# A hybrid attention layer on one core: a new order in the first tile, and the product with the state from f16 pairs

## Chip, core, metric

The kernel runs on one core of one Trainium2 chip. The metric is the device time of one execution in microseconds, the median of several runs. TensorE (PE) multiplies, VectorE (DVE) and ScalarE (ACT) do elementwise work, GpSimd (POOL) does almost nothing here, and SyncE (SP) issues nearly all DMAs.

## What is computed

One layer of an encoder is applied to a prompt of 4096 tokens and to a sample of 64 tokens, in f32, width 1024:

```python
shift, scale, gate = split(silu(c) @ w_ada + b_ada, 3)
h    = rmsnorm(x, g_pre) * (1 + scale) + shift
proj = h @ w_in                 # 2832 columns: gq gk gv gg ga | sq sk sv sg
# GLA: 4 heads, dk 64, dv 128, a gate per token and channel
log_a = log_sigmoid(ga @ w_alpha + b_alpha) / 16
S_t  = diag(exp(log_a_t)) S_{t-1} + k_t^T v_t ;  o_t = q_t S_t
o_gla = rmsnorm(o) * silu(gg)
# SWA: 8 query heads, 2 key heads, window = own and previous chunk of 64, a sink per head
o_swa = softmax_with_sink(rope(sq) rope(sk)^T / 8) sv * silu(sg)
y    = x + gate * rmsnorm(concat(o_gla, o_swa) @ w_out, g_post)
```

Outputs are y for both, the GLA states behind both, and the key and value caches.

## The kernel before

**Tiles.** The prompt is cut into 32 tiles of 128 tokens. Tiles 0 and 1 are written out (`first` and `second` in the program; 0 to 3 on ScalarE), a loop runs two tiles at a time, tiles 30 and 31 are written out again; then come `sample()` and `after()`. Every engine has its own program, an instruction list in a fixed order with waits on named semaphores; nothing is planned by a scheduler.

**Pairs.** A matmul of f32 accuracy is made of f16 pairs: each operand is split into an upper half (`hi`, a copy to f16, mostly on ScalarE) and a lower one (`lo`, the difference, on VectorE), and the three products hi·hi, hi·lo, lo·hi are added in PSUM (`split_product`). The weights are split the same way while they arrive: `split_hi` on ScalarE counts the semaphore `w_half`, `split_lo` on VectorE counts `w_split`. One product was left in f32: q_int times the state S, in `gla_out`, two matmuls of 256 columns a tile; S holds two heads side by side with zeros in the other head's rows.

**A tile on PE**, in order: q and k of GLA (`qk_mm`, 96 matmuls of 128 columns); `gla_out` of the *previous* tile; the projections `W_KSG` (272 columns) and `W_SQ`; a transpose of the gate input; `values` (softmax weights times v) and `state_product` of the previous tile; `W_V`; z; `W_GG`; `W_SG`; the scores; the transposes of k_out and the products q·k of GLA (`a_mm`); the output projection of the previous tile (`out_mm`, 48 matmuls of 512 columns). In tile 0 `modulation(2)`, the gate's part of the adaLN, stands where there is no output projection.

**A tile on VectorE**: `make_h` (h of the next tile), scaling of y, the gates of the previous tile (waits for `o_rs` from ScalarE), the residual, `ga_lo` and `v_lo` (semaphore `vb_lo`, which PE awaits ahead of its transpose), `h_tok_lo`, rope, `mix_swa`, `s_update` (the state), `mix_lo`, `v_keys`, the lower q/k pairs (`pair_lo`), `v_ev`, the gate's running sum `scan`, exponents and factors (`bc_d`, `fac_d`), the scaled q and k (`qk_d`, then `k_off`, `q_int`, `k_out`: `gla_sc`), a copy of the keys (`k_ev`), the gate of gg (add one, reciprocal, multiply: `gg_x`), the maxima of the scores up to `m_neg`, the masking (`a_masked`), the gate of sg (reciprocal; in the middle of it `at_d`, the lower halves of A and k, semaphore that PE awaits ahead of the next tile), `p_lo`, denominators, `sg_g`. Both gates use the one buffer `etmp`.

**ScalarE** makes squares and roots, upper halves, exponentials; near a tile's end: the exponentials of gg and sg, the softmax (8 exponentials), `p_hi`, and then `at_hi`, the upper halves of A and k.

**SyncE** issues in the order of its list. In a tile: store of y, load of the residual, transposes of h (`turn_h`, by DMA), of q and k (`turn_heads`), the load of x for the tile after next, the transposes of the mix (`turn_mix`, which the output projection awaits), of the softmax weights (`turn_probs`). In tile 0 the loads of the last four adaLN units and of w_out stand among these.

Of the kernel before, what the change touches and what calls it, by code (L numbers as in the profile page):

```python
# [29 lines left out]
MID0, MID1 = 32, 96  # L30
P_SHIFT = 15.0 * math.log(2.0)
# [22 lines left out]
UNITS += [("ada", GATE_UNIT + i, slot) for i, slot in enumerate((4, 5, 6, 3))]  # L54
# [32 lines left out]
def hybrid_layer(nc, x_prompt, x_sample, c_prompt, c_sample, state_gla, cache_k, cache_v, w_ada, b_ada, g_pre,  # L87
# [3 lines left out]
    with ctx:  # L91
# [74 lines left out]
        q_int, k_out = lsp, la  # L166
# [6 lines left out]
        S = sb("S", [P, 2, 2, DV])  # L173
# [114 lines left out]
        def _(sp):  # L288
# [56 lines left out]
            def store_state(t, st):  # L345
                sp.wait_ge(sem["s_upd"], t)
                for q in range(2):
                    sp.dma_start(st[0, 0].rearrange("(b q) k v -> q k b v", q=2)[q],
                                 S[DK * q:DK * q + DK, :, q, :]).then_inc(sem["out_stored"], 16)

# [73 lines left out]
            def sample():  # L424
# [8 lines left out]
                for q in range(2):  # L433
                    sp.dma_start(S[DK * q:DK * q + DK, :, q, :],
                                 state_gla[0, 0].rearrange("(b q) k v -> q k b v", q=2)[q]).then_inc(sem["state_in"], 16)
# [46 lines left out]
        def _(pe):  # L482
            def split_product(out, a, b):

                for c in range(KC):
                    for n, (i, j) in enumerate(((0, 0), (0, 1), (1, 0))):
                        last = pe.matmul(out, a(c, i), b(c, j), start=(c == 0 and n == 0),  # L487
                                         stop=(c == KC - 1 and n == 2))
                return last
# [97 lines left out]
            def program(c):  # L587
# [5 lines left out]
                def project(bank, width, col, done):  # L593

                    if c.first:
                        pe.wait_ge(w_split, in_units_before[col])
                    split_product(bank[:, 0:width], h,
                                  lambda cc, i: (w_hi, w_lo)[i][:, cc, col:col + width]).then_inc(done, 1)
# [9 lines left out]
                for b in range(4):  # L608
                    if c.first and b % 2 == 0:
                        pe.wait_ge(w_split, b // 2 + 1)  # L610
                    last = split_product(qk_ch[:, b, :],
                                         lambda cc, i: (w_hi, w_lo)[i][:, cc, W_QK + b * P:W_QK + (b + 1) * P], h)
# [120 lines left out]
            def sample():  # L733
# [62 lines left out]
                pe.wait_ge(sem["state_in"], 16 * 2)  # L796
                for b in range(2):
                    pe.matmul(o_gla_s[:, 2 * b * DV:2 * (b + 1) * DV], q_int[:, b, 0:CHUNK], S[:, b, :, :],
                              start=True, stop=False)
# [70 lines left out]
        def _(act):  # L870
# [108 lines left out]

            def program(c):  # L980
# [38 lines left out]
                if c.first:  # L1019
                    split_hi([("in", 8), ("in", 9)])  # L1020
# [28 lines left out]
                if c.first:  # L1049
                    split_hi([("in", 10), ("in", 11)])  # L1050
# [38 lines left out]
                act.wait_ge(sem["a_masked"], t + 1)  # L1089
                act.activation(aT[0:64, 0, :, :, :], qk_d[0:64, :, :, :], ACT.Copy)  # L1090
                act.activation(aT[64:128, 0, :, :, 64:128], qk_d[64:128, :, :, 64:128], ACT.Copy)
                act.activation(k_tok[:, 0, :, :], kt_ps, ACT.Copy).then_inc(sem["at_hi"], 1)
# [100 lines left out]
        def _(dve):  # L1193
# [116 lines left out]
            def s_update(t):  # L1310
                dve.wait_ge(sem["u_mm"], t)
                for q in range(2):
                    r = slice(DK * q, DK * (q + 1))
                    for b in range(2):
                        last = dve.scalar_tensor_tensor(S[r, b, q, :], S[r, b, q, :], fac[r, b, 5:6],
                                                        u_ps[r, b, :], ALU.mult, ALU.add)
                last.then_inc(sem["s_upd"], 1)

# [26 lines left out]
            def y_scale(n, buf):  # L1345
                dve.wait_ge(sem["y_rs"], n)
                dve.scalar_tensor_tensor(y_buf[buf], pairP[:, :], y_r[:, :], gate_row, ALU.mult, ALU.mult)\
                   .then_inc(sem["y_mul"], 1)

            def program(c):  # L1350
# [39 lines left out]
                if c.prev:  # L1390
# [7 lines left out]
                                      mix_tok[:, :, 0, :], ALU.subtract).then_inc(sem["mix_lo"], 1)  # L1398
                if c.second:
# [8 lines left out]
                if c.first:  # L1408
                    make_h(c)
# [15 lines left out]
                dve.wait_ge(sem["scan"], t + 1)  # L1425
                refs = bsum[:, :, :].rearrange("p b (h k) -> p b h k", h=2)[:, :, :, MID0:MID0 + 1]
# [4 lines left out]
                dve.tensor_copy(fac_in[:, :, 0:2], ref2)  # L1431
# [15 lines left out]
                if c.last:  # L1447
# [4 lines left out]
                dve.tensor_tensor(halves(q_int), halves(q_d),  # L1452
                                  fac[:, :, 0:2].unsqueeze(3).to_broadcast([P, 2, 2, CHUNK]), ALU.mult)
# [12 lines left out]
                dve.wait_ge(sem["gg_e"], t + 1)  # L1466
                dve.tensor_scalar(etmp[:, :], etmp[:, :], 1.0, None, ALU.add).then_inc(sem["gg_1"], 1)
                dve.wait_ge(sem["gg_1"], t + 1)
                dve.reciprocal(etmp[:, :], etmp[:, :]).then_inc(sem["gg_r"], 1)  # L1469
                dve.wait_ge(sem["gg_r"], t + 1)  # L1470
                dve.scalar_tensor_tensor(gates[:, 0:512], bank6[:, :], DESCALE, etmp[:, :], ALU.mult, ALU.mult)\  # L1471
                   .then_inc(sem["gg_x"], 1)

# [28 lines left out]
                for q in range(2):  # L1502
# [5 lines left out]
                last.then_inc(sem["a_masked"], 1)  # L1508

# [4 lines left out]
                dve.wait_ge(sem["at_hi"], t + 1)  # L1514
                dve.tensor_tensor(aT[0:64, 1, :, :, :], qk_d[0:64, :, :, :], aT[0:64, 0, :, :, :], ALU.subtract)
                dve.tensor_tensor(aT[64:128, 1, :, :, 64:128], qk_d[64:128, :, :, 64:128],
                                  aT[64:128, 0, :, :, 64:128], ALU.subtract)
                dve.tensor_tensor(k_tok[:, 1, :, :], kt_ps, k_tok[:, 0, :, :], ALU.subtract).then_inc(sem["at_d"], 1)  # L1518
                dve.wait_ge(sem["sg_r"], t + 1)
                for ch in range(2):  # L1520
# [7 lines left out]
                dve.wait_ge(sem["p_hi"], t + 1)  # L1528
                dve.tensor_tensor(pair_tok[:, 1, :], late[:, 0:D], pair_tok[:, 0, :], ALU.subtract)\
                   .then_inc(sem["p_lo"], 1)  # L1530
# [10 lines left out]
            def sample():  # L1541
# [36 lines left out]
                dve.tensor_copy(fac_in[:, :, 0], bsum[:, :, MID0])  # L1578
# [13 lines left out]
                dve.tensor_tensor(q_int[:, :, c0], q_d[:, :, c0], fac[:, :, 0:1].to_broadcast([P, 2, CHUNK]), ALU.mult)  # L1592
# [11 lines left out]
                dve.tensor_copy(vA_s[c0, :, :], vB[c0, 0, :, :]).then_inc(sem["v_keys"], 1)  # L1604
                dve.wait_ge(sem["a_mm"], t + 1)
# [86 lines left out]
        def _(pool):  # L1692
# [15 lines left out]
            pool.memset(S[:, :, :, :], 0.0).then_inc(sem["scan_m"], 1)  # L1708
# [46 lines left out]
```

## Time and profile before

| | us |
|---|---|
| median of 3 runs | 1537.49 (1537.09 to 1538.28) |
| the profiled execution | 1537.71 |
| its span, first to last instruction | 1536.0 |
| PE busy | 1491.2 (97%) |
| DVE busy | 1151.2 (75%) |
| ACT busy | 634.5 (41%) |
| a tile of the loop | 44.7 |

All times in the views count from the start of the span. A matmul's end is modelled, since matmuls overlap; their starts tell the pace. In the chain of waits each piece is the work that the end waited for at that time.

### The profile page before, as it was taken

The page shows a single profiled execution, that of the slowest core. Times are in us where ns is not written, and L with a number is a line of the kernel's source. Part 1 is how long each engine was busy: PE and PEld are TensorE (multiplying, and loading weights), DVE is VectorE, ACT ScalarE, POOL GpSimd, SP SyncE. Part 2 cuts the span into 40 slices and gives each one's busy share as a digit, 9 for nine tenths or more (in the row PEclk, how much of TensorE's full clock was granted, in tenths as well). Part 3 has the DMA queues.
Part 4 walks back from the last instruction along what each step waited for, and adds up shares of the span by engine and source line. Part 5 has one row for each costly group of instructions (what it writes and reads, how often), then busy time and mean ns, then how long its engine had stood idle before and what let it go on. Part 6 is the DMA issues. An engine that isn't in the chain of part 4 may idle for free.

```text
span 1536.0 us, 31114 instructions
## 1 busy us (share of the span) xinstructions
PE 1491.2 (97%) x12204; PEld 872.2 (57%) x12204; DVE 1151.2 (75%) x2262; ACT 634.5 (41%) x1905; POOL 7.1 (0%) x17
## 2 busy tenths in 40 slices
PE   4789999999999999999999999999999999999997
PEld 3455556566555656655565665556566555656653
DVE  1889877777887777788777778877777887777775
ACT  2735443444444344344434434443443434344343
POOL 1000000000000000000000000000000000000000
PEclk9889999999999999999999999999999999999999
DMA  9982333323233332323333232333323243432334
GB/s 318 302 219 67 89 84 93 81 67 86 58 91 80 92 84 65 89 53 92 79 92 85 65 89 51 92 79 92 89 61 89 51 92 79 92 90 63 68 49 102
DMA packets 305388, 144.53 MB, mean 94 GB/s; under 512 B 266769, under 2 KB 291690, under 8 KB 305354
## 3 DMA queue, kind: packets, MB, share of 16 engines
q1 hardware_dynamic: 304768, 143.92, 38.8%
q8 instruction: 22, 0.36, 0.1%
q10 hardware_dynamic: 586, 0.15, 0.0%
q14 instruction: 12, 0.10, 0.0%
HBM read 63.08 MB, written 17.56 MB: 53 GB/s over the span
## 4 chain that ended last, share of the span: by engine, by line
PE 92%; DVE 4%; DMA 1%; ACT 1%; issue 1%; SPq 0%; ACTq 0%; DVEq 0%
PE bank L487 59%; PE pairP L487 20%; PE pairQ L549 2%; PE pairQ L674 2%; PE pairQ L566 2%; PE pairQ L554 1%; PE pairQ L576 1%; DMA w_hi<-in_w_ada 1%; PE bank L500 1%; PE bank L717 1%; PE bank L652 1%; PE bank L684 1%; DMA hT<-pair_tok 1%; PE bank L680 0%; DVE etmp L1469 0%
## 5 line engine op out<-in xcount | busy, mean ns | idle before, releaser
L487 PE MATMUL bank<-w_hi,hT 128*128 128x512 f16 (+1 forms) x2576 | 719.5, 360 | 7.8 <-DVE w_lo L1236 7.8
L487 PE MATMUL bank<-w_lo,hT 128*128 128x512 f16 (+2 forms) x1288 | 462.9, 359 | 0.0
L487 PEld LDWEIGHTS bank<-w_hi,hT 128*128 128x128 f16 x2576 | 252.5, 98 | 255.3 <-issue 10.1
L487 PE MATMUL pairP<-wo,late 128*128 128x512 f16 x1488 | 326.6, 379 | 0.0
L487 PEld LDWEIGHTS pairP<-wo,late 128*128 128x128 f16 x1488 | 143.0, 98 | 170.4
L487 PE MATMUL bank<-hT,w_hi 128*128 128x128 f16 (+1 forms) x2112 | 182.0, 221 | 10.3 <-DVE k_tok L1518 5.8
L487 PEld LDWEIGHTS bank<-w_lo,hT 128*128 128x128 f16 (+1 forms) x1288 | 126.3, 98 | 114.6 <-issue 0.8
L487 PE MATMUL bank<-hT,w_lo 128*128 128x128 f16 (+1 forms) x1056 | 179.9, 221 | 0.0
L487 PEld LDWEIGHTS bank<-hT,w_hi 128*128 128x128 f16 x2112 | 164.3, 99 | 18.7 <-issue 6.7
L1361 DVE SCALAR_TENSOR_TENSOR gates<-pairQ,o_r,gates 128x128 f32<-128x128 f32 x124 | 34.9, 345 | 109.0 <-ACT o_r L900 109.0
L1079 ACT ACTIVATE late<-pairQ,m_neg 128x128 f32<-128x128 f32 (+1 forms) x256 | 89.6, 376 | 58.9 <-DVE m_neg L1495 58.9
L1469 DVE RECIPROCAL etmp<-etmp 128x512 f32<-128x512 f32 x32 | 107.3, 3353 | 1.1
L1513 DVE RECIPROCAL etmp<-etmp 128x512 f32<-128x512 f32 x32 | 107.3, 3353 | 1.1
L487 PEld LDWEIGHTS bank<-hT,w_lo 128*128 128x128 f16 x1056 | 104.4, 99 | 0.0
L991 ACT ACTIVATE junk<-pairQ 128x128 f16<-128x128 f32 x124 | 32.5, 277 | 165.3 <-PE pairQ L554 165.3
L1069 ACT ACTIVATE etmp<-bank 128x512 f32<-128x512 f32 x32 | 19.1, 597 | 156.3 <-DVE gates L1471 146.3
L1327 DVE TENSOR_TENSOR etmp<-qk_tok,trig_in 128x80 f32<-128x80 f32 (+1 forms) x33 | 8.0, 242 | 93.3 <-ACT qk_tok L1014 93.0
L1014 ACT ACTIVATE qk_tok<-bank 128x512 f32<-128x512 f32 x32 | 19.1, 597 | 112.2 <-PE bank L487 112.2
L975 ACT ACTIVATE stage<-pairP 128x1024 f32<-128x1024 f32 x32 | 32.8, 1024 | 76.6 <-PE pairP L487 75.5
L1025 ACT ACTIVATE pair_tok<-gates 128x1024 f16<-128x1024 f32 x31 | 32.8, 1057 | 66.0 <-DMA hT<-pair_tok 64.3
L1079 ACT ACTIVATION_READ_ACCUMULATOR late<-pairQ,m_neg 128x1 f32 x256 | 55.4, 217 | 0.0
L1525 DVE SCALAR_TENSOR_TENSOR gates<-bank,etmp 64x256 f32<-64x256 f32 x128 | 53.6, 419 | 1.3
(300 smaller groups left out, 1939.4 us busy)
## 6 DMA issues: line engine op xcount, KB each, us to landing
x_in<-in_x_prompt SPq DMA_DIRECT2D x32, 512.0 KB, 3.5
x_res<-in_x_prompt SPq DMA_DIRECT2D x32, 512.0 KB, 4.2
out<-stage SPq DMA_DIRECT2D x32, 512.0 KB, 3.1
wo<-in_w_in SPq DMA_DIRECT2D x8, 1024.0 KB, 11.4
w_hi<-in_w_ada SPq DMA_DIRECT2D x4, 1024.0 KB, 9.1
w_lo<-in_w_ada SPq DMA_DIRECT2D x4, 1024.0 KB, 12.6
wo<-in_w_ada SPq DMA_DIRECT2D x4, 1024.0 KB, 7.3
late<-pair_tok SPq DMA_TRANSPOSE x160, 3.2
```

Source lines behind the costliest of these rows:

```text
L487: last = pe.matmul(out, a(c, i), b(c, j), start=(c == 0 and n == 0), stop=(c == KC - 1 and n == 2))
L549: pe.matmul(o_ps[:, 2 * b * DV:2 * (b + 1) * DV], q_int[:, b, :], S[:, b, :, :], start=True, stop=False)
L566: last = pe.matmul(pv_ps[:, k * HD:(k + 1) * HD], pair_ch[:, i, k, :], v[:, j, HD * g:HD * (g + 1)], start=(n == 0), stop=(n == 2))
L674: last = pe.matmul(scores[:, 4 * g + 2 * ch + pp, :], qT[:, ch, head:head + 2, :], kk[:, g, part, :], start=(part == 0), stop=(part == 1))
L975: act.activation(y_buf[buf], pairP[:, :], ACT.Square, accum_out=y_ss[:, :]).then_inc(sem["y_sq"], 1)
L991: last = act.activation(junk[:, hd * DV:(hd + 1) * DV], o_ps[:, hd * DV:(hd + 1) * DV], ACT.Square, accum_out=o_ss[:, hd:hd + 1])
L1025: act.activation(mix_tok[:, :, 0, :], gates[:, :].rearrange("p (f k) -> p f k", f=2), ACT.Copy)\
L1079: act.activation(probs[:, g, 0:w], scores[:, g, 0:w], ACT.Exp, bias=m_neg[:, g:g + 1], scale=HD ** -0.5, accum_out=row_sum[:, g:g + 1])
L1361: last = dve.scalar_tensor_tensor(gates[:, o], o_ps[:, o], o_r[:, hd:hd + 1], gates[:, o], ALU.mult, ALU.mult)
L1469: dve.reciprocal(etmp[:, :], etmp[:, :]).then_inc(sem["gg_r"], 1)
L1513: dve.reciprocal(etmp[:, :], etmp[:, :]).then_inc(sem["sg_r"], 1)
L1525: last = dve.scalar_tensor_tensor(gates_swa[CHUNK * e:CHUNK * (e + 1), :, ch, :, :], heads[0], DESCALE, heads[1], ALU.mult, ALU.mult)
```

## The change

Two things are changed together.

*State product.* S is kept once, without the zeros (`[P, 2, 128]`), and a pair of f16 halves of S/8 in the layout with zeros (`S_pair`) beside it. `s_hi` and `s_lo` make the halves each tile, `s_hi` behind `mix_lo`, `s_lo` behind the scan. q_int becomes a pair too (upper half, an f32 copy `q_tmp` in the place of bsum, lower half as the difference); the factor 8 is put into its exponent. `gla_out` multiplies three f16 pairs of 256 columns in place of one f32 pair.

*Order.* In tile 0 PE adds all products with the weights' upper halves first and waits for the lower halves (`w_split`) only then. ScalarE splits unit 10 earlier. VectorE's `make_h` goes behind the splits of units 10 and 11; the gate of gg goes behind `p_lo`, ahead of the gate of sg, whose exponential moves behind `p_hi`. In tiles 0 and 1 `at_hi` stands ahead of the softmax and `at_lo` ahead of the gate of sg. The last adaLN unit is loaded into slot 1, not 3.

```diff
+S_SCALE = 8.0
-UNITS += [("ada", GATE_UNIT + i, slot) for i, slot in enumerate((4, 5, 6, 3))]
+UNITS += [("ada", GATE_UNIT + i, slot) for i, slot in enumerate((4, 5, 6, 1))]
...
-        q_int, k_out = lsp, la
+        q_int = lsp[:, :, :].bitcast(F16).rearrange("p b (s k) -> p b s k", s=2)
+        q_tmp, k_out = bsum, la
-        S = sb("S", [P, 2, 2, DV])
+        S = sb("S", [P, 2, DV])
+        S_pair = sb("S_pair", [P, 2, 2, 2, DV], F16)
...
+            def upper_first(out, operands, units):
+                pe.wait_ge(w_half, units)
+                for c in range(KC):
+                    for i in range(2):
+                        pe.matmul(out, *operands(c, i, 0), start=(c == 0 and i == 0), stop=False)
+                pe.wait_ge(w_split, units)
+                for c in range(KC):
+                    last = pe.matmul(out, *operands(c, 0, 1), start=False, stop=(c == KC - 1))
+                return last
...
             def gla_out():
                 for b in range(2):
-                    pe.matmul(o_ps[:, 2 * b * DV:2 * (b + 1) * DV], q_int[:, b, :], S[:, b, :, :],
-                              start=True, stop=False)
+                    for n, (i, j) in enumerate(((0, 0), (0, 1), (1, 0))):
+                        pe.matmul(o_ps[:, 2 * b * DV:2 * (b + 1) * DV], q_int[:, b, i, :], S_pair[:, j, b, :, :],
+                                  start=(n == 0), stop=False)
```

ScalarE:

```diff
                 if c.first:
-                    split_hi([("in", 8), ("in", 9)])
+                    split_hi([("in", 8), ("in", 9), ("in", 10)])
...
                 if c.first:
-                    split_hi([("in", 10), ("in", 11)])
+                    split_hi([("in", 11)])
...
-                act.wait_ge(sem["sg_mm"], t + 1)
-                act.wait_ge(sem["gg_x"], t + 1)
-                act.activation(etmp[:, :], bank7[:, :], ACT.Exp, scale=-DESCALE).then_inc(sem["sg_e"], 1)
+                if not c.first:
+                    sg_exp(t)
+                if c.first or c.second:
+                    at_hi(t)
                 act.wait_ge(sem["m_neg"], t + 1)
...
                 act.activation(pair_tok[:, 0, :], late[:, 0:D], ACT.Copy).then_inc(sem["p_hi"], 1)
...
+                if c.first:
+                    sg_exp(t)
+                if not (c.first or c.second):
+                    at_hi(t)
```

VectorE (`gg_gate`, `at_lo`, `p_lo` hold the lines that stood in the program, unchanged):

```diff
+            def s_hi():
+                for q in range(2):
+                    r = slice(DK * q, DK * (q + 1))
+                    last = dve.tensor_scalar(S_pair[r, 0, :, q, :], S[r, :, :], 1.0 / S_SCALE, None, ALU.mult)
+                return last
+
+            def s_lo():
+                for q in range(2):
+                    r = slice(DK * q, DK * (q + 1))
+                    last = dve.scalar_tensor_tensor(S_pair[r, 1, :, q, :], S[r, :, :], 1.0 / S_SCALE,
+                                                    S_pair[r, 0, :, q, :], ALU.mult, ALU.subtract)
+                return last
...
                     dve.tensor_tensor(mix_tok[:, :, 1, :], gates[:, :].rearrange("p (f k) -> p f k", f=2),
                                       mix_tok[:, :, 0, :], ALU.subtract).then_inc(sem["mix_lo"], 1)
+                    dve.wait_ge(sem["s_upd"], t)
+                    s_hi()
...
                    .then_inc(sem["pair_lo"], 1)
-                if c.first:
-                    make_h(c)
...
                 dve.wait_ge(sem["scan"], t + 1)
+                if c.prev:
+                    s_lo()
...
-                dve.tensor_copy(fac_in[:, :, 0:2], ref2)
+                dve.tensor_scalar(fac_in[:, :, 0:2], ref2, TAU * math.log(S_SCALE), None, ALU.add)
...
                 if c.first:
                     split_lo([("in", 10), ("in", 11)])
+                    make_h(c)
...
-                dve.tensor_tensor(halves(q_int), halves(q_d),
-                                  fac[:, :, 0:2].unsqueeze(3).to_broadcast([P, 2, 2, CHUNK]), ALU.mult)
+                by_half = fac[:, :, 0:2].unsqueeze(3).to_broadcast([P, 2, 2, CHUNK])
+                dve.tensor_tensor(q_int[:, :, 0, :].rearrange("p b (h k) -> p b h k", h=2), halves(q_d), by_half,
+                                  ALU.mult)
+                dve.tensor_tensor(halves(q_tmp), halves(q_d), by_half, ALU.mult)
...
                 dve.tensor_copy(kA[:, :, :, 0:CHUNK], kB[:, :, :, 0:CHUNK]).then_inc(sem["k_ev"], 1)
+                dve.wait_ge(sem["gla_sc"], t + 1)
+                dve.tensor_tensor(q_int[:, :, 1, :], q_tmp[:, :, :], q_int[:, :, 0, :], ALU.subtract)
                 if c.first:
                     h_tok_lo(c)
...
+                if not c.first:
+                    gg_gate(t)
...
                 last.then_inc(sem["a_masked"], 1)
+                if c.first or c.second:
+                    at_lo(t)
+                if c.first:
+                    p_lo(t)
+                    gg_gate(t)
```

The sample on VectorE, behind `a_masked` and behind the reciprocal, and POOL:

```diff
+                dve.wait_ge(sem["state_in"], 16 * 2)
+                s_hi().then_inc(sem["state_in"], 1)
...
+                dve.wait_ge(sem["state_in"], 16 * 2 + 1)
+                s_lo().then_inc(sem["state_in"], 1)
                 dve.wait_ge(sem["sc_mm"], t + 1)
...
+            pool.memset(S_pair[:, :, :, :, :], 0.0)
+            pool.memset(S[:, :, :], 0.0).then_inc(sem["scan_m"], 1)
```

In the sample the state is loaded by a DMA into S (`state_in`), PE's product there uses the pairs as in `gla_out`, and q_int is made as in a tile.

## Rows read from the trace of the kernel before

**Rows 1.** The page: busy time of the engines, and the chain that ended last.

```profile
PE 1491.2 (97%) x12204; PEld 872.2 (57%) x12204; DVE 1151.2 (75%) x2262; ACT 634.5 (41%) x1905; POOL 7.1 (0%) x17
...
PE 92%; DVE 4%; DMA 1%; ACT 1%; issue 1%; SPq 0%; ACTq 0%; DVEq 0%
```

**Rows 2.** Stretches: length, busy PE, PEld, DVE, ACT, POOL (x), PEclk, DMA share, GB/s.

```profile
95.00:100.00 5.00, 5.00 (x64) 5.00 (x62) 4.78 (x8) 0.00 (x0) 0.00 (x0) 0.66 0.96 355
233.50:278.20 44.70, 44.70 (x367) 26.07 (x365) 33.92 (x68) 18.28 (x57) 0.00 (x0) 1.00 0.34 79
847.00:848.00 1.00, 1.00 (x18) 0.88 (x17) 0.40 (x1) 0.51 (x1) 0.00 (x0) 1.00 0.00 0
1505.00:1506.00 1.00, 1.00 (x12) 0.41 (x8) 0.03 (x1) 0.00 (x0) 0.00 (x0) 1.00 0.00 0
```

**Rows 3.** Who waited for whom: us in total, times, longest.

```profile
PE bank L487 <- DVE w_lo L1236: 7.8, 3, 5.3
PE bank L487 <- DVE k_tok L1518: 5.8, 2, 4.6
```

**Rows 4.** The chain of waits in order of time: start, us, what.

```profile
94.38 7.15 PE bank L487 x96
...
103.17 2.79 PE bank L487 x24
...
143.92 5.52 PE bank L487 x96
...
194.16 0.49 PE pairQ L549 x2
194.64 0.33 PE pairQ L554 x6
...
849.08 10.47 PE pairP L487 x48
...
1506.97 0.48 DVE qk_d L1608 x2
```

**Rows 5.** Timeline of VectorE in tiles 0 and 1: start, us, operation, [idle before].

```profile
67.44 1.28 DVE L1264 SCALAR_TENSOR_TENSOR late<-x_in,x_r,xs 128x1024 f32<-128x1024 f32 x1
...
76.71 0.42 DVE L1440 SCALAR_TENSOR_TENSOR qk_d<-bank,qk_d 128x256 f32<-128x256 f32 x1
...
79.79 0.42 DVE L1467 TENSOR_SCALAR etmp<-etmp 128x512 f32<-128x512 f32 x1
80.24 3.35 DVE L1469 RECIPROCAL etmp<-etmp 128x512 f32<-128x512 f32 x1
...
85.42 0.17 DVE L1478 MEMSET late<- 128x128 f32 x1 [1.10 <-PE pairQ L674]
...
98.15 1.28 DVE L1264 SCALAR_TENSOR_TENSOR late<-x_in,x_r,xs 128x1024 f32<-128x1024 f32 x1
...
104.95 1.13 DVE L1361 SCALAR_TENSOR_TENSOR gates<-pairQ,o_r,gates 128x128 f32<-128x128 f32 x4 [4.26 <-ACT o_r L900]
```

**Rows 6.** Timeline of ScalarE in tile 0: softmax, p_hi, at_hi.

```profile
87.44 0.32 ACT L1079 ACTIVATE late<-pairQ,m_neg 128x64 f32<-128x64 f32 x1 [2.37 <-DVE m_neg L1495]
...
90.25 1.06 ACT L1088 ACTIVATE pair_tok<-late 128x1024 f16<-128x1024 f32 x1
91.22 0.61 ACT L1090 ACTIVATE aT<-qk_d 64x512 f16<-64x512 f32 x1
```

**Rows 7.** Timeline of VectorE in a tile of the loop.

```profile
832.16 1.23 DVE L1315 SCALAR_TENSOR_TENSOR S<-S,fac,pairQ 64x128 f32<-64x128 f32 x4
...
837.17 0.69 DVE L1414 SCALAR_TENSOR_TENSOR v_raw<-bank,v_raw 128x512 f16<-128x512 f32 x1 [0.46 <-ACT v_raw L1037]
...
842.02 0.42 DVE L1452 TENSOR_TENSOR lsp<-qk_d,fac 128x256 f32<-128x256 f32 x1
...
848.23 0.69 DVE L1484 TENSOR_REDUCE smax<-pairQ 128x4 f32<-128x512 f32 x1 [0.83 <-PE pairQ L674]
...
856.55 0.42 DVE L1518 TENSOR_TENSOR k_tok<-bank,k_tok 128x256 f16<-128x256 f32 x1
```

More of the change, by code:

```diff
@@ L608, in program @@
                 for b in range(4):
[L609 to L612, printed above, removed]
+                    cols = slice(W_QK + b * P, W_QK + (b + 1) * P)
+                    if c.first:
+                        last = upper_first(qk_ch[:, b, :], lambda cc, i, j: ((w_hi, w_lo)[j][:, cc, cols], h(cc, i)),
+                                           b // 2 + 1)
+                    else:
+                        last = split_product(qk_ch[:, b, :], lambda cc, i: (w_hi, w_lo)[i][:, cc, cols], h)
                 last.then_inc(sem["qk_mm"], 1)
@@ L795, in sample @@
                 pe.wait_ge(sem["p_exp"], t + 1)
-                pe.wait_ge(sem["state_in"], 16 * 2)
+                pe.wait_ge(sem["state_in"], 16 * 2 + 2)
                 for b in range(2):
-                    pe.matmul(o_gla_s[:, 2 * b * DV:2 * (b + 1) * DV], q_int[:, b, 0:CHUNK], S[:, b, :, :],
-                              start=True, stop=False)
+                    for n, (i, j) in enumerate(PRODUCTS):
+                        pe.matmul(o_gla_s[:, 2 * b * DV:2 * (b + 1) * DV], q_int[:, b, i, 0:CHUNK],
+                                  S_pair[:, j, b, :, :], start=(n == 0), stop=False)
                     for q in range(2):
@@ L1348, in y_scale, with p_lo, gg_gate, at_lo @@
                    .then_inc(sem["y_mul"], 1)
+            def p_lo(t):
+                dve.wait_ge(sem["p_hi"], t + 1)
+                dve.tensor_tensor(pair_tok[:, 1, :], late[:, 0:D], pair_tok[:, 0, :], ALU.subtract)\
+                   .then_inc(sem["p_lo"], 1)
+            def gg_gate(t):
+                dve.wait_ge(sem["gg_e"], t + 1)
+                dve.tensor_scalar(etmp[:, :], etmp[:, :], 1.0, None, ALU.add).then_inc(sem["gg_1"], 1)
+                dve.wait_ge(sem["gg_1"], t + 1)
+                dve.reciprocal(etmp[:, :], etmp[:, :]).then_inc(sem["gg_r"], 1)
+                dve.wait_ge(sem["gg_r"], t + 1)
+                dve.scalar_tensor_tensor(gates[:, 0:512], bank6[:, :], DESCALE, etmp[:, :], ALU.mult, ALU.mult)\
+                   .then_inc(sem["gg_x"], 1)
+            def at_lo(t):
+                dve.wait_ge(sem["at_hi"], t + 1)
+                dve.tensor_tensor(aT[0:64, 1, :, :, :], qk_d[0:64, :, :, :], aT[0:64, 0, :, :, :], ALU.subtract)
+                dve.tensor_tensor(aT[64:128, 1, :, :, 64:128], qk_d[64:128, :, :, 64:128],
+                                  aT[64:128, 0, :, :, 64:128], ALU.subtract)
+                dve.tensor_tensor(k_tok[:, 1, :, :], kt_ps, k_tok[:, 0, :, :], ALU.subtract).then_inc(sem["at_d"], 1)
             def program(c):
@@ L1508, in program @@
                 last.then_inc(sem["a_masked"], 1)
+                if c.first or c.second:
+                    at_lo(t)
+                if c.first:
+                    p_lo(t)
+                    gg_gate(t)
                 dve.wait_ge(sem["sg_e"], t + 1)
@@ L1513, in program @@
                 dve.reciprocal(etmp[:, :], etmp[:, :]).then_inc(sem["sg_r"], 1)
[L1514 to L1518, printed above, removed]
+                if not (c.first or c.second):
+                    at_lo(t)
                 dve.wait_ge(sem["sg_r"], t + 1)
@@ L1527, in program @@
                 last.then_inc(sem["sg_x"], 1)
-                dve.wait_ge(sem["p_hi"], t + 1)
-                dve.tensor_tensor(pair_tok[:, 1, :], late[:, 0:D], pair_tok[:, 0, :], ALU.subtract)\
-                   .then_inc(sem["p_lo"], 1)
+                if not c.first:
+                    p_lo(t)
                 dve.wait_ge(sem["p_exp"], t + 1)
@@ L1604, in sample @@
                 dve.tensor_copy(vA_s[c0, :, :], vB[c0, 0, :, :]).then_inc(sem["v_keys"], 1)
+                dve.wait_ge(sem["gla_sc"], t + 1)
+                dve.tensor_tensor(q_int[:, :, 1, c0], q_tmp[:, :, c0], q_int[:, :, 0, c0], ALU.subtract)
                 dve.wait_ge(sem["a_mm"], t + 1)
```

37 lines of the change are left out of this document (19 added, 18 removed).

## The prediction

> **What bounds the kernel now.** I read the shares of the chain that ended last first, then the busy time by stretch, then that chain in order of time, then who waited for whom, and last the VectorE and ScalarE timelines of the first two tiles and of one tile of the loop. TensorE (PE) carries 92% of the chain and is busy 97% of the span [rows 1]. In a tile of the loop it is busy for all 44.70 us of 44.70 while VectorE (DVE) works 33.92 [rows 2]: from about 144 us on, a microsecond saved on PE is a microsecond of the kernel, and work added to DVE is free as long as no PE wait comes to end late. Ahead of that it is otherwise: PE waits 7.8 us for the lower halves of the weights and 5.8 us for DVE's `k_tok` [rows 3], which is the end of the work that hands a tile over (semaphore `at_d`). After the second of these waits the clock falls: 0.66 of full speed between 95 and 100 us [rows 2], and the same 96 matmuls take 7.15 us where they take 5.52 at tile 2 [rows 4]. So there are three terms: the loop (PE), the first two tiles (DVE and ScalarE in turn with PE), and the end (the sample, where the chain runs through DVE).
>
> **The state product, in the loop.** One f32 matmul of 256 columns (two records) takes 0.49 us on the chain, and six f16 ones of 128 columns take 0.33, or 0.056 each [rows 4]. The change puts three f16 matmuls of 256 columns in place of each. No such row exists. Two of 128 columns would be 0.112; the 24 matmuls of 272 columns take 2.79 us, 0.116 each, which is an upper end, and scaled by 256/272 they give 0.109 [rows 4]. I take 0.110, so 0.33 in place of 0.49: 0.16 saved, with ends 0.14 and 0.163. There are two products a tile, and PE sets the time at 31 of the 32 places (tiles 2 to 31 and the sample; tile 1 belongs to the front). 62 x 0.16 = **9.9 us less** (8.7 to 10.1). Their weights are as wide as those of the other f16 matmuls, whose loads lie under matmuls half as long.
>
> The row is dearer than a count of passes makes it: four passes at 0.110 would be 0.44, and 62 x 0.11 only 6.8 us. That count is the Trainium skill's, "FP8 and Floating Point Precision", section "TensorE Precision Notes": a true FP32 product goes through the array four times. By that rule three passes in place of four save a quarter; the trace, with 0.49 us, says a third. The measurement decides, and the quarter is a rival below.
>
> **What DVE pays for it in the loop.** New per tile: `s_hi` (two one-source operations on 64x256), `s_lo` (two two-source ones), `q_tmp`, and the lower half of `q_int`. A two-source operation of 256 elements lasts 0.42 us and its successor starts 0.34 later [rows 7]; a one-source f32 operation of 512 elements lasts 0.42, one of 256 therefore between 0.15 and 0.42 [rows 5]; I take 0.25 apart. Sum: 0.5 + 0.7 + 0.34 + 0.34 = 1.9 us (1.7 to 2.3). The scaled copy into `fac_in` costs what the copy did. Cover, in order. `s_hi` stands ahead of `v_keys` and the lower q/k pairs, so the pairs end 0.5 late; SyncE's queue holds their transposes ahead of `turn_mix`, so the transposes of the mix end 0.5 late too. They were over by 847, since no DMA ran from 847 to 848 [rows 2], and PE wants them at 849.08 [rows 4]: 2 us of cover. `v_ev` takes 0.46 us of idle time in front of it [rows 7], which eats the 0.5. `s_lo` (0.7) delays the exponentials, `q_tmp` and the lower half come behind: 1.4 us at the gate of `gg`. The maximum over the scores waits 0.83 for PE [rows 7], so 0.55 is left, and `at_d`, now at 856.97, comes at 857.5 where PE asks for it at 849.08 + 10.47 = 859.55 [rows 4, 7]. Everything is hidden, with some 2 us to spare. Cost taken: nothing.
>
> **Tile 0.** Upper halves first: PE no longer waits for w_split at `W_V` and `W_GG`, and at `W_SG` only with its last 8 matmuls. DVE's operations up to the q/k products are only reordered (`make_h`, 2.5 us, goes behind the last two splits), so it reaches them at 76.7 as before [rows 5], and `k_ev`, one `q_tmp` later, at 79.1. PE, done with `W_SG` at 76.1, waits there: the 7.8 us saved are kept only as far as DVE allows, and scores run 79.1 to 80.0. The gg gate (0.45 + 3.35 + 0.7 us) leaves this place [rows 5, 7], so after `h_tok_lo` the work on the scores starts at 80.5 in place of 85.42. Masking ends at 84.0, `at_hi` (1.4, ahead of the softmax) at 85.4, `at_lo` at 87.0, where PE's wait for it ended at 94.38 [rows 4]: tile 1 could start 7.3 us earlier. But what was put off is still DVE's: it waits 2.4 us for softmax (2.8) and p_hi (1.06) on ScalarE [rows 6], then p_lo 1.15, the gg gate 4.5, 0.7 for the exponential of sg, which needs the same buffer, and sg and the rest 6.6: 102.3, where tile 1's `make_h` started at 98.15 [rows 5]. DVE is 4.15 us **later** into tile 1.
>
> **Tile 1.** DVE there waited 4.26 us for ScalarE's `o_r` [rows 5]; with PE early that wait is gone. The gates start at 104.85 (104.95 before). PE has to wait for `vb_lo` at 106.3, four microseconds or so; a fallen clock may cost 1.6 us, as in the 7.15 us block [rows 4], and `W_V` has 3 us until ScalarE wants it. From there on ScalarE and DVE set the pace: about 1.6 us come from the transposes of h, no longer behind the loads of w_out, and from small waits; the new 1.9 us go back; and `at_hi` ahead of the softmax takes out 2.81 + 1.06 us of ScalarE, part of it now DVE's reciprocal [rows 6]. I arrive at `at_d` at 141.0 in place of 143.9 [rows 4]: 2.8 us. In tile 2 DVE is behind by what it put off (reciprocal, sg, p_lo), and its pairs come 3 us later behind PE than in the loop; the transposes of the mix have 2 us of cover less 0.5, so PE waits about 1.4 us before the output product. From tile 3 on this is made up. Front: **1.4 us less**, between 3.5 less (no wait in tile 2 and a little more gained) and 1.5 more (nothing won in tile 1, and the wait).
>
> **The end.** In the sample the chain goes from the masking at 1506.97 straight along DVE [rows 4]. `s_hi` and `s_lo` stand in that stretch: 0.5 + 0.75, **1.25 us more** (0.9 to 1.6). They also wait for the new state, but no DMA runs from 1505 to 1506 [rows 2], so it has landed. `q_tmp` and its pair lie under the wait for PE there. POOL's second memset lies in its long idle time.
>
> **Sum.** -9.9 - 1.4 + 1.25 = -10.05 us against the profiled execution, 1537.71 us (span 1536.0 and 1.71 around it): 1527.7. The median of the runs is 0.2 lower, so I say **1527.5 us**.
>
> **Rivals.**
> *A quarter, not a third.* If the 0.05 us that an f32 matmul takes beyond four passes comes back in another form (weight loads that show between 256-column matmuls), the product saves 6.8 and the kernel takes 1530.5. Against: no wait stands between matmuls of 272 columns, and the chain is solid there [rows 4].
> *The front gives everything back.* DVE's put-off work delays tile 2 by more than tile 1 won: +1.5 for the front gives 1530.4. For it: 4.15 us of lateness at tile 1. Both together: 1533.
> *The front keeps more.* No wait in tile 2, PE's start of tile 2 at 140: 1524 to 1525.5.
> *Slower.* In each tile the transposes of the mix land after PE wants them, because `s_hi` pushes the pairs and so SyncE's queue. Cover is 2 us and the saving 0.32 a tile, so it decides where `s_hi` costs more than 2.3 us; at 2.6, 31 x (0.6 - 0.32) - 1.4 + 1.25 gives 1546, and between 2.2 and 2.4 the time is about the old one. Against: the four operations of `s_update`, next to it, take 1.23 in all [rows 7], and it has two.
> *The change doesn't do what it says* (f16 no quicker than f32): excluded by the 0.33 for six.
>
> **Chances.** Forecast (1525.5 to 1530): 0.62. Front keeps more: 0.13. A quarter, or the front gives back, or both (1530 to 1534): 0.16. No change or slower by the loop: 0.09. Range 1523.5 to 1531.5: it leaves out the slower cases, the sum of both mishaps, and the far end of the front. 0.2% of 1537.5 is 3.1 us, about what a measurement of this kernel can tell from no change: faster 0.91, same 0.05, slower 0.04.
>
> **What would show it.** Tile period 44.38 in place of 44.70 with PE still solid; the product at 0.33 on the chain; `at_d` of tile 0 near 87, tile 1's `make_h` near 102, PE's tile 2 near 141, a PE wait of 1 to 2 us at the output product of tile 2; 1.2 us more between the masking and the maxima in the sample. A period that stays at 44.7 with a wait at `turn_mix`'s transposes or at `at_d` would prove the cover wrong; a tile 2 start after 144 the front.

## The result and the profile after

The changed kernel takes 1530.57 us (median of 5 runs, 1528.87 to 1531.55), beside 1537.09 us for the kernel before (median of 5, 1536.93 to 1538.28): ratio 0.995, 95% interval 0.9937 to 0.9963. It is faster, by 6.5 us, where 10 were forecast. The time lies above the band that the prediction gave its forecast (1525.5 to 1530) and inside its wider range (up to 1531.5); it came out near the rival "the front gives everything back" (1530.4). The profiled execution is the slowest of the five (1531.55), and the one before took 1537.71.

The page of the changed kernel, its busy time and the chain that ended last, which answers to [rows 1]:

```profile
PE 1482.3 (97%) x12270; PEld 868.5 (57%) x12270; DVE 1214.8 (79%) x2456; ACT 635.9 (42%) x1905; POOL 7.8 (1%) x18
...
PE 86%; DVE 7%; DMA 3%; ACT 2%; issue 1%; SPq 1%; DVEq 0%; ACTq 0%
```

PE works 8.9 us less in all, and still its share of the chain falls from 92% to 86%: DVE, the DMAs and SyncE's queue have come onto it. Where, the chain in order of time tells (start, us, what; to be read beside [rows 4]):

```profile
178.02 12.16 PE pairP L490 x48
190.19 5.36 PE bank L490 x96
...
856.13 5.36 PE bank L490 x96
861.50 0.33 PE pairQ L564 x3
...
1433.29 5.36 PE bank L490 x96
...
1478.88 2.96 PE bank L490 x96
```

Three f16 matmuls now take 0.33 us where the f32 one took 0.49. The rows of 96 matmuls are the starts of tiles and of the sample. The same places before (output product of tile 2, then the starts of tile 3, of tile 31 and of the sample):

```profile
178.33 10.47 PE pairP L487 x48
188.80 5.36 PE bank L487 x96
...
1440.86 5.36 PE bank L487 x96
...
1486.45 2.80 PE bank L487 x96
```

This cuts the difference of the two spans (1529.8 - 1536.0 = -6.2) into four pieces:

| piece | forecast | measured | how |
|---|---|---|---|
| up to the start of tile 3 | -1.72 (front -1.4, one tile's product -0.32) | +1.39 | 190.19 - 188.80 |
| tiles 3 to 30 | -8.96 (28 x 0.32) | -8.96 | 1243.10 - 1252.06 |
| tile 31 | -0.32 | 0.00 | 45.59 both |
| sample | +0.93 (1.25 - 0.32) | +1.37 | 50.92 - 49.55 |

Of the 3.85 us that are missing, 3.1 lie before tile 3, 0.3 in tile 31 and 0.45 in the sample. Stretches of the changed kernel (columns as in [rows 2]): the begin of the output product of tile 2, its first 3 us alone, and a tile of the loop.

```profile
178.00:182.00 4.00, 3.98 (x11) 1.49 (x12) 3.86 (x12) 2.41 (x12) 0.00 (x0) 0.58 0.00 0
...
178.00:181.00 3.00, 2.98 (x8) 1.06 (x9) 2.91 (x9) 1.41 (x6) 0.00 (x0) 0.50 0.00 0
...
190.00:234.39 44.39, 44.39 (x366) 26.00 (x365) 34.92 (x74) 18.33 (x57) 0.00 (x0) 1.00 0.35 81
```

In the loop PE is busy for all 44.39 us, as before for 44.70. In tile 2 PE had waited 2.0 us, and behind that the granted clock was 0.50 for the first 3 us (the lower of its two levels, 1.2 of 2.4 GHz) and 0.58 over 4 us; the 48 matmuls of the output product took 12.16 us where 10.47 is usual [rows 4]. What came ahead of that is in PE's waits between 60 and 200 us:

```profile
PE bank L654 <- DVE vB L1339: 4.6, 1, 4.6
...
PE pairP L490 <- DMA late<-pair_tok: 2.0, 1, 2.0
```

and in tile 2 on SyncE, ScalarE and VectorE, one fence each:

```profile
155.80 0.37 SPq L397 DMA_DIRECT2D out<-stage  x1
156.36 0.37 SPq L398 DMA_DIRECT2D x_res<-in_x_prompt  x1
156.97 3.88 SPq L380 DMA_TRANSPOSE hT<-pair_tok  x2
167.43 2.51 SPq L389 DMA_TRANSPOSE qT<-etmp  x2
...
172.53 1.25 SPq L357 DMA_TRANSPOSE late<-pair_tok  x1
173.83 2.70 SPq L360 DMA_TRANSPOSE late<-pair_tok  x2
```

```profile
152.16 1.06 ACT L990 ACTIVATE pair_tok<-late 128x1024 f16<-128x1024 f32 x1
...
163.00 1.06 ACT L1056 ACTIVATE pair_tok<-gates 128x1024 f16<-128x1024 f32 x1 [5.45 <-DMA hT<-pair_tok]
```

```profile
154.39 1.22 DVE L1433 TENSOR_TENSOR stage<-stage,x_res 128x1024 f32<-128x1024 f32 x1
...
164.09 1.22 DVE L1463 TENSOR_TENSOR pair_tok<-gates,pair_tok 128x1024 f16<-128x1024 f32 x1 [3.61 <-ACT pair_tok L1056]
...
166.93 0.42 DVE L1474 TENSOR_TENSOR junk<-qk_tok,junk 128x256 f16<-128x256 f32 x1
```

Read from the end: PE waits for the transposes of the mix (L357, L360), which stand in SyncE's queue behind those of the q/k pairs, which wait for L1474. That is late because DVE waits 3.61 us at L1463 for ScalarE, and ScalarE waits 5.45 us at L1056, since it may not write into `pair_tok` before the transposes of h (L380) have read it. Those are issued at 156.97 only. The upper half of h was ready at 153.2 (L990), but the store of y (L397) stands ahead of them in the queue, and it waits for the residual (L1433), which ends at 155.6, behind the work that tile 1 put off (the gate of sg, `p_lo`). This chain through the queue is not in the prediction. It stood in the kernel before, too, and at nearly the same times; SyncE in its tile 2:

```profile
156.48 3.68 SPq L377 DMA_TRANSPOSE hT<-pair_tok  x2
...
171.03 1.25 SPq L354 DMA_TRANSPOSE late<-pair_tok  x1
```

But there PE asked for its end at 178.33. The change brings PE to that place 2.3 us earlier, and the transposes of the mix 1.5 us later.

### The profile page after: what moved, and what is told of

Same layout as the page of the kernel before. It is cut to its first block, busy times and chain, and to the rows that moved or that the text cites. A ratio compares the mean times of both kernels' runs of the same rounds, so it can differ in the third digit from the quotient of the medians.

```text
span 1529.8 us, 31441 instructions
## 1 busy us (share of the span) xinstructions
PE 1482.3 (97%) x12270; PEld 868.5 (57%) x12270; DVE 1214.8 (79%) x2456; ACT 635.9 (42%) x1905; POOL 7.8 (1%) x18
## 3 DMA queue, kind: packets, MB, share of 16 engines
q1 hardware_dynamic: 304768, 143.92, 38.6%
## 4 chain that ended last, share of the span: by engine, by line
PE 86%; DVE 7%; DMA 3%; ACT 2%; issue 1%; SPq 1%; DVEq 0%; ACTq 0%
PE bank L490 54%; PE pairP L490 20%; PE pairQ L693 2%; PE pairQ L581 2%; PE pairQ L569 1%; PE pairQ L564 1%; DVE w_lo L1268 1%; PE pairQ L591 1%; DMA w_hi<-in_w_ada 1%; PE bank L514 1%; DMA stage<-in_w_in 1%; PE bank L736 1%; DVE etmp L1404 1%; PE bank L671 1%; DVE wo L1263 1%
## 5 line engine op out<-in xcount | busy, mean ns | idle before, releaser
L490 PE MATMUL bank<-w_hi,hT 128*128 128x272 f16 (+2 forms) x2496 | 696.6, 359 | 0.0
L490 PE MATMUL bank<-w_lo,hT 128*128 128x272 f16 (+2 forms) x1248 | 448.2, 359 | 0.0
L490 PEld LDWEIGHTS bank<-w_hi,hT 128*128 128x128 f16 (+1 forms) x2496 | 244.6, 98 | 239.2 <-issue 1.8
L490 PEld LDWEIGHTS bank<-w_lo,hT 128*128 128x128 f16 (+1 forms) x1248 | 122.4, 98 | 111.1 <-issue 0.8
L490 PE MATMUL bank<-hT,w_hi 128*128 128x128 f16 (+1 forms) x2048 | 172.4, 218 | 1.8 <-DVE k_tok L1414 1.8
L490 PE MATMUL bank<-hT,w_lo 128*128 128x128 f16 (+1 forms) x1024 | 170.7, 218 | 0.0
L490 PEld LDWEIGHTS bank<-hT,w_hi 128*128 128x128 f16 x2048 | 156.5, 98 | 10.0 <-DMA hT<-pair_tok 1.8
L490 PEld LDWEIGHTS bank<-hT,w_lo 128*128 128x128 f16 x1024 | 99.9, 98 | 0.0
L1056 ACT ACTIVATE pair_tok<-gates 128x1024 f16<-128x1024 f32 x31 | 32.8, 1058 | 70.5 <-DMA hT<-pair_tok 65.1
```

What stands on the lines that cost most here:

```text
L1056: act.activation(mix_tok[:, :, 0, :], gates[:, :].rearrange("p (f k) -> p f k", f=2), ACT.Copy)\
```

## Experiments

**Each half of the change by itself.** The diff of the change, split at its two headings: the state product in the old order, and the new order with the f32 product.

> The f16 state product alone, in the order of the kernel before. Theory A (the loop is worth -0.32 us a tile, and the work that the product adds to VectorE in tiles 0 and 1, about 2 us, makes the hand-over to tile 2 late, with nothing to give it back): 28 tiles from tile 3 on at -0.32 = -9.0, tile 3 begins 1 to 1.5 us later than the 188.80 of before, the sample +1.2: 1530.0 to 1531.5, the same as both changes together. Rival B (the new order is what lost the time in the changed kernel, and without it the product keeps all it saves): 1537.1 - 9.9 + 1.5 = 1528.5 to 1529, tile 3 at 188.5.

> The new order of tiles 0 and 1 alone, with the f32 state product. Theory A (the order wins 3 to 4 us at the hand-over to tile 2, and it is the product's work on VectorE and the late transposes of the mix in tile 2 that eat it): tile 2 begins near 140, the output product of tile 2 waits under 0.5 us, its clock stays full, tile 3 near 185 in place of 188.80: 1533 to 1534.5. Rival B (the order by itself gives nothing or costs, since what it puts off is paid in tile 2): tile 3 at 188.8 to 190.2, 1537 to 1538.5.

Product alone: 1533.70 us (6 runs, 1531.62 to 1536.43), ratio 0.997 (0.9958 to 0.9982). Order alone: 1534.15 us (9 runs, 1533.28 to 1535.26), ratio 0.9977 (0.9967 to 0.9987). The chains around tile 2, product alone first:

```profile
146.40 7.15 PE bank L490 x96
...
182.12 10.47 PE pairP L490 x48
192.59 5.36 PE bank L490 x96
```

```profile
174.73 10.53 PE pairP L487 x48
185.26 5.36 PE bank L487 x96
```

The order alone brings tile 3 forward by 3.54 us, with 0.26 of wait in tile 2, and its time lies where theory A had it. The product alone makes tile 3 later by 3.79 us, more than A's 1 to 1.5, and its time lies above A's 1530.0 to 1531.5: its work on VectorE brings the hand-over from 143.92 to 146.40, and PE, after 2.6 us of waiting there, does the 96 matmuls in 7.15 us, not 5.52. So the product costs the front 4.1 us (its own 0.32 counted), and the two halves don't add: -3.5 and +3.8 in the front give +1.39 together, since the early hand-over of the order meets a tile 2 that cannot use it. Rival B of the first run, that the order lost the time, is out. The profiled execution of the product alone is the slowest of its six (1536.43); 2.7 us of that lie in the sample, which takes 53.6 us in place of 50.9. The 3.8 and the 4.1 are figures of this one execution.

**Tile 1 in the old order.** Only tile 0 keeps A and k ahead of the softmax:

```diff
-                if c.first or c.second:
+                if c.first:
                     at_hi(t)
```

(and the same for `at_lo`).

> The changed kernel with the upper and lower halves of A and k of tile 1 behind the softmax again (tile 0 as changed). Theory A (the early hand-over of tile 1 is taken back in tile 2 by a wait at the output product, and the fallen clock behind the wait costs 1.7 us on top): tile 2 begins near 144, no wait and a full clock at its output product (10.47 us), tile 3 near 188.8, 1529 to 1529.5. Rival B (the early hand-over is worth what it wins, 2 us, and the wait has another cause that stays): tile 3 at 191 to 192, 1532.

Measured: 1531.50 us (5 runs, 1529.48 to 1532.13), ratio 0.9953 (0.994 to 0.9967).

```profile
144.03 7.15 PE bank L490 x96
...
179.74 10.47 PE pairP L490 x48
190.21 5.36 PE bank L490 x96
```

The wait and the slow output product are gone, as A said, but its 188.8 for tile 3 and its 1529 to 1529.5 are missed: PE now waits 2.6 us for the hand-over itself, and the clock falls there (7.15 us). Tile 3 begins when it did, 190.2. Moving the wait from one place to the other is worth nothing.

**The transposes of h first in SyncE's queue.**

```diff
+                if c.prev and not c.last:
+                    turn_h(c)
                 if c.prev2:
                     sp.wait_ge(sem["y_final"], c.t - 1)
...
-                if c.prev and not c.last:
-                    turn_h(c)
```

> The changed kernel with the transposes of h ahead of the store of y and the load of the residual in SyncE's queue, in every tile. Theory A (in tile 2 the store waits for VectorE's residual, which is late by what was put off, and holds up the transposes of h, and by them ScalarE's upper halves of the mix, VectorE for 3.6 us and the transposes of the mix): these land 1.5 to 2.5 us earlier, the wait of 2.0 us at the output product of tile 2 shrinks to under 0.6 and the clock stays full: tile 3 near 186.7, 1526.5 to 1528. Rival B (VectorE is late by itself, the queue is no cause): wait and clock as they are, 1530.5. In the loop neither expects a change, period 44.39.

Measured: 1529.41 us (5 runs, 1527.49 to 1530.01), ratio 0.9941 (0.9927 to 0.9955). SyncE in tile 2, and the chain:

```profile
153.03 5.03 SPq L380 DMA_TRANSPOSE hT<-pair_tok  x2
158.36 0.37 SPq L399 DMA_DIRECT2D out<-stage  x1
...
169.47 1.24 SPq L357 DMA_TRANSPOSE late<-pair_tok  x1
```

```profile
175.77 10.47 PE pairP L490 x48
186.24 5.36 PE bank L490 x96
```

VectorE is where it was (residual at 154.11), the first transpose goes out 3.9 us earlier, those of the mix 3.1 us, and PE's wait and the slow clock are both gone: tile 3 at 186.24, 3.95 us earlier than in the changed kernel. The queue was the cause, and VectorE's lateness by itself cost nothing in tile 2. This is read from the trace: the intervals of the two ratios overlap, so the times alone don't tell this run from the changed kernel. The total misses A's 1526.5 to 1528 by 1.4. In the profiled execution (span 1526.6, 3.2 us less) part of it was given back in the sample, where PE waited 2.5 us for the softmax and the products behind ran slower.

**The end.** Both halves of the sample's state made in VectorE's wait ahead of the masking, and the store of the last tile's keys and values ahead of the transposes of its pairs (the same lines leave their old places):

```diff
+                dve.wait_ge(sem["state_in"], 16 * 2)
+                s_hi().then_inc(sem["state_in"], 1)
+                dve.wait_ge(sem["state_in"], 16 * 2 + 1)
+                s_lo().then_inc(sem["state_in"], 1)
                 dve.wait_ge(sem["a_mm"], t + 1)
...
+                if c.last:
+                    store_kv(c.t, P, k_prompt[0, 0], v_prompt[0, 0])
                 turn_heads(c)
```

> The changed kernel with two edits at its end: the halves of the state in the sample made in the wait ahead of the masking, and the store of keys and values of the last tile ahead of the transposes of its q/k pairs. Theory A (both halves lie on VectorE's chain in the sample, 1.51 us between masking and maxima more than before, and the longer wait of PE for the softmax there lets the clock fall in some executions; the wait of 2.25 us for the store delays the hand-over of tile 31 by 0.3): masking to m_neg back to 5.2 us, PE's wait ahead of the sample's state product back to about 1.0, no wait for k_tok at the sample: 1528.5 to 1529.2. Rival B (the state arrives from memory too late for the new place, so the wait moves to the masking): 1530 to 1531.

Measured: 1527.76 us (5 runs, 1527.60 to 1530.24), ratio 0.9938 (0.9924 to 0.9951). VectorE's timeline in the sample, and the stretch at the output product of tile 2:

```profile
1494.98 0.58 DVE L1354 TENSOR_SCALAR S_pair<-S 64x256 f16<-64x256 f32 x2
1495.60 0.85 DVE L1360 SCALAR_TENSOR_TENSOR S_pair<-S,S_pair 64x256 f16<-64x256 f32 x2
1496.81 0.48 DVE L1684 TENSOR_TENSOR qk_d<-bank,causal 64x128 f32<-64x128 f32 x2 [0.36 <-PE bank L795]
...
1501.79 0.17 DVE L1698 TENSOR_SCALAR m_neg<-m_pos 128x8 f32<-128x8 f32 x1
```

```profile
177.70:181.70 4.00, 3.98 (x19) 1.86 (x20) 3.86 (x12) 2.35 (x12) 0.00 (x0) 1.00 0.00 0
```

The result lies below A's range. The halves fit, with 0.36 us of the wait left. From the masking to `m_neg`, the end of the maxima, it is 4.98 us from start to start (1496.81 to 1501.79), as before (4.99), and 6.49 in the changed kernel. Tile 31 takes 45.27 us, 0.32 less. That is 1.8 us, and the result is better by 2.8: in tile 2 of this execution PE waited 1.6 us and the clock stayed at 1.00 (10.53 us for the 48 matmuls), so tile 3 began at 188.25. That part is not the edit's.

**Both together**, the transposes first and the end:

> The transposes of h first in SyncE's queue, and both edits at the end. Theory A (the front's 3.9 us and the end's 1.4 add, and without the longer wait in the sample the clock stays up there): tile 3 near 186.2, masking to m_neg 5.2, 1525.5 to 1526.8. Rival B (one takes the other's gain, as product and order did): 1528 to 1529.

Measured: **1525.90 us** (5 runs, 1525.47 to 1526.04), ratio 0.992 (0.9907 to 0.9934). Tile 2 begins at 141.90, its output product at 175.99 without a wait, tile 3 at 186.46, and a tile of the loop takes 44.40. The gains add, as A said. This is the best version, 4.7 us under the changed kernel, and its interval lies clear of that one's.

**The order taken out of it.** The same with the old order of tiles 0 and 1:

> The product in the old order of tiles 0 and 1, with the transposes of h first in SyncE's queue and both edits at the end: what is left of turn_h_first_tail when the new order is taken out. Theory A (the order is worth its 3.5 us and more once nothing takes them back, since without it the hand-over to tile 2 comes at 146.4 and the clock falls there): tile 2 at 146.4, tile 3 at 192.5, 1531 to 1532.5. Rival B (the queue's order alone mends the front, the new order is not needed): tile 3 near 188, 1527 to 1528.

Measured: 1531.59 us (5 runs, 1530.84 to 1533.15), ratio 0.9958 (0.9944 to 0.9971); tile 2 at 147.52, after 2.6 us of waiting for the hand-over, tile 3 at 193.71, each about 1 us later than A said. So the new order is worth 5.7 us by the two medians, once SyncE's queue lets tile 2 use it. The two versions were measured in different series, in which the kernel before took 1537.41 and 1538.53; each against its own, it is 4.6 us.

**A fourth product.**

```diff
-                    for n, (i, j) in enumerate(((0, 0), (0, 1), (1, 0))):
+                    for n, (i, j) in enumerate(((0, 0), (0, 1), (1, 0), (1, 1))):
```

> The changed kernel with a fourth f16 product, lower times lower half, in the state product of every tile (the sample keeps three). Theory A (each f16 matmul of 256 columns costs 0.110 us, passes simply add): period 44.39 + 0.22 = 44.61, 0.44 in place of 0.33 on the chain, 1530.6 + 31 x 0.22 = 1537.4, so that even four passes are under the 0.49 of f32. Rival B (the f32 matmul costs 0.49 because of four passes and what surrounds a product, so four f16 passes cost 0.49 too): period 44.71, 1540.5.

Measured: 1536.60 us (11 runs, 1535.86 to 1539.17), ratio 0.9995 (0.9986 to 1.0004). On the chain, two starts of a tile with the products of the first:

```profile
857.09 5.36 PE bank L490 x96
862.45 0.44 PE pairQ L564 x4
...
901.71 5.36 PE bank L490 x96
```

Four passes take 0.44 us and the period is 44.62, as A said: each matmul costs the 0.110 that the prediction took, and passes simply add.

**The cover in the loop.** Four maxima behind `s_hi`:

```diff
                     s_hi()
+                    for n in range(4):
+                        dve.tensor_reduce(spare[:, n, :], gates[:, 0:512].rearrange("p (f k) -> p f k", f=4),
+                                          AX_X, ALU.max)
```

> The changed kernel with four maxima over 128x512 behind the upper half of the state, in every tile from 1 to 31, whose results nobody reads: some 2.4 us of VectorE more at the place where the prediction saw 2 us of cover, less 0.5. Theory A (the transposes of the mix have 1.5 us left in a tile of the loop): PE waits 0.9 us at the output product of each tile, period 45.3 if the clock stays full, 1530.6 + 29 x 0.9 = 1557, and more if the clock falls behind each wait. Rival B (the cover is larger than read, VectorE catches up in its idle 20%): period 44.39, 1531 to 1533, the rest in tiles 1 and 2 only.

Measured: 1567.04 us (4 runs, 1565.50 to 1570.20), ratio 1.0185 (1.017 to 1.0201). PE's waits in the whole run (us, times, longest), and a stretch of 46 us in the loop:

```profile
PE pairP L491 <- DMA late<-pair_tok: 31.8, 30, 2.3
```

```profile
891.00:937.00 46.00, 45.04 (x383) 26.40 (x380) 38.90 (x81) 18.30 (x57) 0.00 (x0) 1.00 0.35 81
```

Each tile waits, 1.06 us in the mean, at the place that the rival "slower" named, and the period is 45.42 in this tile (875.52 to 920.94), 45.49 in the mean. The four maxima take 2.46 us, so the cover that the change had left is 1.4 us; the prediction had it at 2 less 0.5. VectorE idles for 7 of 46 us and still can't make it up, since its order is fixed. The clock stays at 1.00 from 200 to 1400 us. A's 1557 is missed by 10: the tiles lose 1.1 us each and not 0.9, and in the profiled execution (1570.20) tile 3 begins 4.0 us later than in the changed kernel and the sample takes 3.0 us longer, which A did not count.

**The upper half on ScalarE**, in the best version, behind the upper halves of the pairs; `s_lo` waits for it.

```diff
                 act.activation(k_pair[:, :, 0, :, :], k_twice, ACT.Copy).then_inc(sem["pair_hi"], 1)
+                if c.prev:
+                    act.wait_ge(sem["s_upd"], t)
+                    for q in range(2):
+                        r = slice(DK * q, DK * (q + 1))
+                        last = act.activation(S_pair[r, 0, :, q, :], S[r, :, :], ACT.Copy, scale=1.0 / S_SCALE)
+                    last.then_inc(sem["s_hi"], 1)
...
-                    dve.wait_ge(sem["s_upd"], t)
-                    s_hi()
```

> turn_h_first_tail with the upper half of the state made by ScalarE behind the upper halves of the pairs, no longer by VectorE (the sample's stays on VectorE). Theory A (tile 1 is set by VectorE, so its 0.6 us there come off the hand-over to tile 2, and in a tile of the loop the work was hidden on either engine): tile 2 at 141.3, tile 3 at 185.9, period 44.39, 1525.3. Rival B (ScalarE becomes late with its next work, the upper half of v, and VectorE waits for that): tile 2 at 141.9 or later, 1525.9 to 1527.

Measured: 1527.35 us (5 runs, 1526.21 to 1527.94), ratio 0.993 (0.9917 to 0.9944). VectorE in tile 1:

```profile
120.36 2.36 DVE L1269 SCALAR_TENSOR_TENSOR wo<-wo 128x1024 f16<-128x1024 f32 x2 [1.28 <-ACT wo L947]
```

By the trace rival B was right, though with other work than it named: ScalarE's upper halves of w_out come 1 us later, VectorE waits 1.28 us for them, and tile 2 begins at 142.78 in place of 141.90. What VectorE gives away in tile 1 it gets back as a wait. The two times themselves say little: 1.45 us apart by the medians, 0.3 when each is taken against the kernel before of its own series.

## Why the prediction came out as it did

The range held, but the forecast's own band did not: the loop was right, and the 3.85 us that are missing lie ahead of tile 3 and at the end.

*The state product* was right to the row: 0.33 in place of 0.49, period 44.39 (forecast 44.38), 8.96 us in 28 tiles. The fourth product shows 0.44 for four f16 passes, beside 0.49 for the f32 matmul before, and so the rival "a quarter" falls. The rule weighed against the forecast, the four passes of a true FP32 product (the Trainium skill, "FP8 and Floating Point Precision", section "TensorE Precision Notes"), would by the same 0.110 a pass make f32 cost 0.44, an estimate; it leaves 0.05 us a product unexplained, and no run here shows where they go.

*VectorE's cost in the loop* was hidden, as forecast. The new operations came out a little dearer: `s_hi` 0.60 to its successor's start, `s_lo` 0.87, the two on q_int 0.34 each, 2.15 in place of 1.9. The cover ahead of the transposes of the mix was read rightly (1.4 measured, 1.5 forecast), and the four maxima show that it was no formality.

*Tiles 0 and 1* went as described: `at_d` of tile 0 ended at 87.40 (forecast 87.0), `make_h` of tile 1 came at 102.88 (102.3), PE waited 4.6 us for `vb_lo` (4), and `at_d` of tile 1 ended at 141.81 (141.0).

```profile
86.98 0.42 DVE L1414 TENSOR_TENSOR k_tok<-bank,k_tok 128x256 f16<-128x256 f32 x1
...
102.88 1.28 DVE L1296 SCALAR_TENSOR_TENSOR late<-x_in,x_r,xs 128x1024 f32<-128x1024 f32 x1
...
141.39 0.42 DVE L1414 TENSOR_TENSOR k_tok<-bank,k_tok 128x256 f16<-128x256 f32 x1
```

The 0.8 us here are as much as the 0.6 that were there at `make_h` and the 0.25 by which the new operations were sized too small; that these are the cause is argued.

*Tile 2* is the step that failed: "PE waits about 1.4 us before the output product", from which the front was to keep 1.4 us. By the prediction's own terms the transposes were to land at 176.5: 141.0, 34.1 us of PE work up to the output product (178.33 - 143.92 = 34.41 before, less 0.32), and the 1.4. They landed at 178.0, 1.5 us later: PE came to the place about 1 us late, and waited 2.0. A wait near the forecast size did come, but by another way than forecast, and that is luck: the prediction put it down to the late q/k pairs on VectorE and a cover of 2 us, and with the transposes of h first in the queue and VectorE unchanged PE doesn't wait at all. Two things were missing. One is the way the lateness takes: not only VectorE's list, but the store of y in SyncE's queue, ScalarE's 5.45 us behind it, and VectorE again. I had counted what VectorE put off, and not what waits for it in a queue of another engine. Taking the store out of the way brought the transposes 3.1 us forward with VectorE's residual where it was, so this is shown. The other is the clock: I had granted it a place behind the wait in tile 1, where DVE sets the pace anyway (0.63 from 105 to 110 us, behind the 4.6 us), and none behind the wait in tile 2, where every slow matmul counts: 12.16 - 10.47 = 1.7 us. The 1.5 and the 1.7 are, to 0.1, the 3.1 us that are missing.

*The end* was undersized: 1.50 us between masking and `m_neg` in place of 1.25, for the two halves with their gaps. Masking and `m_neg`, in the changed kernel, and `m_neg` before, where the masking stands at 1506.97 [rows 4]:

```profile
1499.22 0.48 DVE L1680 TENSOR_TENSOR qk_d<-bank,causal 64x128 f32<-64x128 f32 x2 [1.75 <-PE bank L795]
...
1505.71 0.17 DVE L1698 TENSOR_SCALAR m_neg<-m_pos 128x8 f32<-128x8 f32 x1
```

```profile
1511.96 0.17 DVE L1622 TENSOR_SCALAR m_neg<-m_pos 128x8 f32<-128x8 f32 x1
```

The 96 matmuls at the sample's start add 0.16 (2.96 for 2.80). And a third of a microsecond was lost in tile 31, where VectorE waits 2.25 us for the store of the cache (0.65 before), an edge that the prediction did not look at. That store takes 3.5 us from issue to landing in the changed kernel and some 1.7 before; why is not shown. Both losses are gone in the run that moves the halves and the store.

What stays open is when the clock falls. At the output product of tile 2 it fell behind 2.0 us and stayed up behind 1.3 (four products), 1.6 (the end) and 2.3 (the maxima); at the hand-over to tile 2 it fell in all three runs that waited 2.6 us. The spread of the changed kernel's own runs (2.7 us), beside 0.6 for the best version without these waits, fits with a fall in some executions and not in others; the run with the upper half on ScalarE, without these waits too, spreads over 1.7, which doesn't. So this is not shown.

## What to carry to other kernels

When an engine's order is changed so that another can start earlier, follow the put-off work through every queue that waits for it, in the next tile too: here the gain of two microseconds was held up by a store that stood in front of a transpose, and swapping the two brought tile 3 forward by 3.95 us. A saving in the steady loop can be taken from one row and multiplied, but its price in the tiles that are bound by another engine has to be worked out there; the same operations that were free in the loop cost 4.1 us in tiles 0 to 2 in the old order, 2.5 by a later hand-over and 1.6 by the clock behind it. Work that must be done once fits best into a wait that is already there, as both halves of the state did in the sample.

## What the runs showed of the hardware

A short wait of TensorE can cost nearly its own length again in clock: behind 2.0 us of wait the granted clock was 0.58 over 4 us, 0.50 (1.2 of 2.4 GHz) in the first 3, and 1.7 us were lost. But a wait of 2.3 us at the same place in the run with the maxima left it at 1.00, and so did that run's other 29 waits, 1.0 us in the mean, one in each tile. On ScalarE the two copies of 64x256 f32 to f16 took 0.82 us, where VectorE needed 0.58.
